# Two linear layers change places, the last attention slots run beside the first of them, and twelve modulation sums are dealt out anew

## The reference, cut to what matters

```
mod = c_act @ w_mod + b_mod                      # 3 x 2048 per layer: shift, scale, gate
h = rms_norm(x, g_norm) * (1 + scale) + shift
rq, rk, rv, rg, cq, ckv, kr, mg, bg = split(h @ w_in)
o_ret = head_group_norm(retention(rope(rq), rope(rk), rv))
y_ret = (o_ret * silu(rg)) @ w_ret_proj          # job "retproj"
q  = rms_norm(cq) @ w_uq ; kv = rms_norm(ckv) @ w_ukv
o_mla = mla_attention(q, kv, kr)                 # 16 heads
y_mla = (o_mla * silu(mg)) @ w_mla_proj          # job "mlaproj"
g_a, g_b = split(sigmoid(bg))                    # jobs "ga" and "gb0".."gb3"
x = x + gate * ((g_a * y_ret + g_b * y_mla) @ w_out)   # job "out"
```

## Time and profile before

| What | Value |
|---|---|
| Median of 3 runs | 3378.76 us (3378.43 to 3387.96) |
| The profiled execution | 3377.11 us, of which its span is 3375.4 us |
| PE busy | 3165.9 us, 94% of the span |
| DVE, ACT busy | 66%, 44% |
| Mean granted PE clock | 0.976 of full |
| Moved by DMA | 650.13 MB, mean 193 GB/s |

### The profile page before, as it was taken

One profiled execution on the slowest core, in us unless ns is written; L12 is line 12 of the kernel. 1 busy time (PEld: TensorE's weight loads), 2 busy tenths in 40 slices (PEclk: granted clock), 3 DMA queues, 4 the chain that ended last, 5 costly groups with the idle time before them and its releaser, 6 DMA issues. The chain is left out here.

```text
span 3375.4 us, 51760 instructions
## 1 busy us (share of the span) xinstructions
PE 3165.9 (94%) x20984; PEld 2734.9 (81%) x20984; DVE 2237.6 (66%) x2653; ACT 1480.8 (44%) x1843; POOL 108.0 (3%) x206
## 2 busy tenths in 40 slices
PE   6999997999989799999999999989999999999997
PEld 5898886878878688888877778868888887777886
DVE  7687877687674668677766667764555765565564
ACT  5454543344453333344444444433334544444443
POOL 0000000000000000000000000000000000000000
PEclk9999998999999899999999999989999999999999
DMA  5334764767544366656653467645544554344543
GB/s 209 127 112 147 260 245 167 280 249 264 187 160 153 145 219 256 235 213 242 244 187 134 149 250 288 217 181 176 179 157 162 188 199 173 127 150 176 212 175 112
DMA packets 102889, 650.13 MB, mean 193 GB/s; under 512 B 11552, under 2 KB 12704, under 8 KB 38688
## 3 DMA queue, kind: packets, MB, share of 16 engines
q1 hardware_dynamic: 71856, 512.44, 42.3%
q0 software_dynamic: 28528, 105.92, 8.7%
q10 hardware_dynamic: 2304, 28.84, 2.1%
HBM read 632.47 MB, written 14.68 MB: 192 GB/s over the span
## 5 line engine op out<-in xcount | busy, mean ns | idle before, releaser
L1562 PE MATMUL acc<-xs,whi 128*128 128x512 f32 x6960 | 2501.1, 403 | 76.3 <-DVE xs L983 60.2
L1564 PE MATMUL acc<-xs,wlo 128*128 128x256 f32 x6960 | 1957.1, 281 | 0.0
L1562 PEld LDWEIGHTS acc<-xs,whi 128*128 128x128 f32 x6960 | 1315.2, 189 | 407.5 <-issue 59.5
L903 DVE TENSOR_TENSOR wlo<-raw,whi 128x2048 fp32r<-128x2048 f32 x459 | 1051.8, 2292 | 502.0 <-ACT whi L444 501.4
L1564 PEld LDWEIGHTS acc<-xs,wlo 128*128 128x128 f32 x6960 | 1322.8, 190 | 6.2 <-issue 3.6
L444 ACT ACTIVATE whi<-raw 128x2048 fp32r<-128x2048 f32 x459 | 875.2, 1907 | 0.0
L468 ACT ACTIVATE acctmp<-acc 128x256 f32<-128x256 f32 x547 | 208.8, 383 | 1349.6 <-PE acc L1564 1331.4
L953 DVE TENSOR_TENSOR w<-acc,acctmp 128x256 f32<-128x256 f32 (+1 forms) x480 | 206.2, 430 | 462.9 <-ACT acctmp L468 462.3
L925 DVE SCALAR_TENSOR_TENSOR modacc<-modw,cact,modacc 128x1024 f32<-128x1024 f32 x192 | 245.6, 1279 | 16.0 <-DMA modw<-in_modstream 14.7
L423 POOL DMA_DIRECT2D modw<-in_modstream x192 | 101.5, 529 | 1709.7 <-DVE modacc L925 1037.4
L529 ACT ACTIVATE smx<-smx,stat 128x128 f32<-128x128 f32 x96 | 43.0, 448 | 175.6 <-DVE stat L1056 175.6
(11 more groups left out here) (256 smaller groups left out, 2181.9 us busy)
## 6 DMA issues: line engine op xcount, KB each, us to landing
raw<-in_wstream SPq DMA_DIRECT2D x483, 1024.0 KB, 4.8
modw<-in_modstream POOLq DMA_DIRECT2D x192, 512.0 KB, 4.7
residual<-h ACTq DMA_DIRECT2D x2, 2048.0 KB, 6.3
ga_gate<-w ACTq DMA_DIRECT2D x2, 2048.0 KB, 10.9
gated_retention<-w ACTq DMA_DIRECT2D x2, 2048.0 KB, 8.5
w<-gated_retention ACTq DMA_DIRECT2D x2, 2048.0 KB, 8.2
h<-residual ACTq DMA_DIRECT2D x2, 2048.0 KB, 12.6
w<-ga_gate ACTq DMA_DIRECT2D x2, 2048.0 KB, 11.3
```

The costliest lines, as they stand in the source:

```text
L903: dve.tensor_tensor(out=wlo[s % SPL][:, :], in0=raw[s % RAW][:, :], in1=whi[s % SPL][:, :].bitcast(F32), op=ALU.subtract).then_inc(w_lo_do ...
L1562: pe.matmul(acc[par % 2][0:cols, :], whi[w][:, c:c + cols], x_split[:, k, :, :], start=(k == 0), stop=False, skip_group_check=True)
L1564: mm = pe.matmul(acc[par % 2][0:cols, 0:T], wlo[w][:, c:c + cols], x_split[:, k, 0, :], start=False, stop=(k == kts - 1), skip_group_check ...
```

## The change

1. In both layers `retproj` stands ahead of `mlaproj` in the job list and in memory.
2. The gated retention comes back into `h`, the residual's buffer, from the start of `gb3`. `gb3` is now `held` and splits `retgated` ahead beside its last block.
3. Slots 15 to 17 run beside blocks 0 to 2 of `retproj`; `mlagated` is split ahead beside the last block of `retproj`.
4. The residual comes back into `h` at block 2 of `retproj`; `ga` comes back at block 5 in four loads of 512 KB into four buffers `ga_w` (on the space of the finished attention); the sigmoid of `gb` moves to blocks 6 to 9. The merge beside `mlaproj` first weights the retention result with `ga`, later adds the other one.
5. The 12 modulation chunks: `foxz` and layer 0's `rg` have none any more; layer 1's `rv` and `mg` have one each. Layer 0's `retproj` and `mlaproj` each keep one. The wait of the modulation matmuls on stored attention heads goes with `foxz`.

```
-              + [("mlaproj", 16), ("retproj", 16), ("out", 16)])
+              + [("retproj", 16), ("mlaproj", 16), ("out", 16)])
...
-MOD_JOBS = [(None, n) for n in ("glu", "s5out", "k", "v", "q", "foxz")] + \
-           [(0, n) for n in ("rv", "ga", "rg", "mg", "mlaproj", "retproj")]
+MOD_JOBS = [(None, n) for n in ("glu", "s5out", "k", "v", "q")] + \
+           [(0, n) for n in ("rv", "ga", "mg", "retproj", "mlaproj")] + [(1, "rv"), (1, "mg")]
...
+        ga_w = [at(f"ga_w{g}", [P, 4, T], F32, o) for g, o in enumerate((o_cr, o_cr + 4 * K, o_cr + 8 * K, o_stg))]
... ACT:
-                attend_slot(a0, MLA_H - 1, MLA_H)
-                attend_slot(a0, MLA_H, MLA_H)
-                act.wait_ge(acc_done, JOBS[(l, "mlaproj")][1])
-                for g in range(4):
-                    act.wait_ge(sem("att_stored"), a0 + 4 * g + 4)
-                    act.activation(xs[:, 4 * g:4 * g + 4, 0, :], group(w2)(g), ACT.Copy).then_inc(x_hi_done, 1)
...
+                act.dma_start(h[:, :, :], away["gated_retention"]).then_inc(sem("gated_back"), 16)
+                project((l, "gb3"), side=before_last(lambda j: attend_slot(a0, MLA_H - HG + j - 1, MLA_H), ret_early, HG - 1),
+                        held=True)
+                split_x(f"retgated{l}", group(h), xs, JOBS[(l, "retproj")][1], (3,))
+                split_held((l, "gb3"))
+                def back_side(j):
+                    if j < 2:
+                        attend_slot(a0, MLA_H - 1 + j, MLA_H)
+                    if j == 2:
+                        act.wait_ge(x_lo_done, SPLIT_BEFORE[f"retgated{l}"] + 4)
+                        act.dma_start(h[:, :, :], away["residual"]).then_inc(sem("residual_back"), 16)
+                    if j == 5:
+                        act.wait_ge(sem("att_stored"), a0 + MLA_H)
+                        act.wait_ge(sem("ga_away"), 16 * (l + 1))
+                        for g in range(4):
+                            act.dma_start(ga_w[g][:, :, :], group(away["ga_gate"])(g)).then_inc(sem("ga_back"), 16)
+                    if 6 <= j < 10:
+                        act.activation(group(w3)(j - 6), group(w3)(j - 6), ACT.Sigmoid).then_inc(sem("gb_gate"), 1)
... PE:
-            project((None, "foxz"), xs, side=fox_slot, before_mod=(sem("att_stored"), FOX_H - 2))
+            project((None, "foxz"), xs, side=fox_slot)
...
-                for k in range(MLA_H - 1, MLA_H + 2):
-                    mla_slot(k)
-                project((l, "mlaproj"), xs, fresh=f"mlagated{l}", before_mod=(sem("att_stored"), a0 + MLA_H), side=unrolled)
-                project((l, "retproj"), xs, fresh=f"retgated{l}", side=unrolled)
+                def slot_side(j):
+                    if j < 3:
+                        mla_slot(MLA_H - 1 + j)
+                project((l, "retproj"), xs, fresh=f"retgated{l}", side=slot_side, before_mod=(sem("att_stored"), a0 + MLA_H))
+                project((l, "mlaproj"), xs, fresh=f"mlagated{l}", side=unrolled)
```

More of the change, by code:

```diff
@@ L113 @@
 NSQUARES = {n: k for n, k, _ in NORMS}
-RELEASES = [(None, "glu"), (None, "f")] + [(l, n) for l in range(2) for n in ("mlaproj", "retproj")]
+RELEASES = [(None, "glu"), (None, "f")] + [(l, n) for l in range(2) for n in ("gb3", "retproj", "mlaproj")]
 OVER = {n: f for n, _, f in NORMS}
@@ L313, in released, with before_last @@
             return 3 * RELEASES.index(key) + g + 1
-        def before_last(side, early):
+        def before_last(side, early, last=KT - 1):
             def at_block(j):
@@ L319, in at_block @@
                     side(j)
-                if j == KT - 2:
+                if j == last - 1:
                     early()
@@ L867, in back_side @@
[L867 to L876, removed]
+                    if g < MLA_G - 1:
+                        project((l, f"gb{g}"), side=lambda j: attend_slot(a0, HG * g + j - 1, MLA_H))
@@ L877, in ret_early @@
                 def ret_early():
                     act.wait_ge(sem("gated_back"), 16 * (l + 1))
[L879 to L887, removed]
@@ L890, in _ @@
+                project((l, "retproj"), side=before_last(back_side, lambda: split_x(
+                    f"mlagated{l}", group(w2), xs, 0, range(3), (l, "retproj"))), held=True)
+                split_x(f"mlagated{l}", group(w2), xs, JOBS[(l, "mlaproj")][1], (3,))
+                split_held((l, "retproj"))
+                project((l, "mlaproj"), side=before_last(None, lambda: split_x(
+                    f"merged{l}", group(w1), xs, 0, range(3), (l, "mlaproj"))))
                 split_x(f"merged{l}", group(w1), xs, JOBS[(l, "out")][1], (3,))
@@ L1483, in ret_early @@
                 def ret_early():
-                    last_mod_step((l, "mlaproj"))
                     dve.wait_ge(sem("gated_back"), 16 * (l + 1))
                     for g in range(3):
-                        split_x(f"retgated{l}", group(w2), xs, g)
-                project((l, "mlaproj"), lambda j: tile(w1, j), side=before_last(None, ret_early), held=True)
-                split_x(f"retgated{l}", group(w2), xs, 3)
-                split_held((l, "mlaproj"))
-                dve.wait_ge(acc_summed, JOBS[(l, "retproj")][1])
+                        split_x(f"retgated{l}", group(h), xs, g)
@@ new lines, in _, with mla_early @@
+                project((l, "gb3"), lambda j: w3[:, MLA_H - HG + j, :],
+                        side=before_last(lambda j: mla_slot(MLA_H - HG + j - 1), ret_early, HG - 1), held=True)
+                split_x(f"retgated{l}", group(h), xs, 3)
+                split_held((l, "gb3"))
+                def mla_early():
+                    last_mod_step((l, "retproj"))
+                    for g in range(3):
+                        split_x(f"mlagated{l}", group(w2), xs, g)
+                def slot_side(j):
+                    if j < 3:
+                        mla_slot(MLA_H - 1 + j)
+                    if j == 3:
+                        dve.wait_ge(sem("att_stored"), a0 + MLA_H)
@@ L1493, in merge_side @@
+                project((l, "retproj"), lambda j: tile(w1, j), side=before_last(slot_side, mla_early), held=True)
+                split_x(f"mlagated{l}", group(w2), xs, 3)
+                split_held((l, "retproj"))
+                dve.wait_ge(acc_summed, JOBS[(l, "mlaproj")][1])
+                dve.wait_ge(x_lo_done, SPLIT_BEFORE[f"mlagated{l}"] + 4)
                 def merge_side(j):
+                    if j == 0:
+                        dve.wait_ge(sem("ga_back"), 64 * (l + 1))
                     if j < 4:
-                        dve.wait_ge(sem("gb_gate"), 4 * l + j + 1)
```

42 lines of the change are left out of this document (20 added, 22 removed).

## The result

The changed kernel takes 3351.62 us (median of 4 runs, 3350.19 to 3356.67) against 3378.60 (4 runs, 3375.82 to 3387.96): a ratio of 0.9913, 95% interval 0.9894 to 0.9932. The forecast was 3353, range 3343 to 3367.

A forecast was written before the change was run, and what follows sets the result against it. PE was busy 94% of the span, so gains were expected mainly where PE waits or runs at its lower clock. Terms -8.7 + 0.5 - 1.3 - 8.2 - 7.3 + 1.0 = -24.0 took 3377.1 to 3353 us, range 3343 to 3367.

The forecast's parts named there:

- Term 1: End of rg, layer 0: losing its modulation chunk removes PE's idle and lower clock; -8.7 us, ends -10 and -7.
- Term 2: rv and mg of layer 1: one added chunk each, hidden under blocks; +0.5 us for both, ends -1 and +3.
- The rival that the chunks cost 2 x 8.7 there: rv and mg, layer 1: moved chunks cost what rg's did, 2 x 8.7 us, giving 3370.0 us; chance 0.05.
- Term 3: End of foxz: without its chunk's modulation matmuls, slots 16 and 17 come earlier; -1.3 us, ends -3 and 0.
- Term 4: From gb3 to retproj's fourth block: attention's tail runs beside retproj; -8.2 us in layer 0, -7.3 in layer 1.
- Seams between the projections: Transitions retproj to mlaproj and mlaproj to out: same splits, held block and chunk as before; 0 us.
- pace: Plain blocks run at 5.55 or 5.65 us, cause unknown; small mean loss expected, +1.0 us, ends -5 and +5.
- The wait at the seam: Rival, gb3 to retproj: fourth group 4 us later, PE at lower clock for a block; 3364.7 us, chance 0.11.
- The late load: Rival, gb3: 2 MB retention load into h lands too late, slower than before; 3389 us at 49 us landing, chance 0.03.
- The faster pace: Rival: jobs behind the change fall into the 5.55 us block pace, giving 3345 us; chance 0.04.

The follow-up runs named there:

- the chunks alone: The kernel before with only the modulation chunks dealt out anew, mlaproj still ahead of retproj: 3371.11 us, ratio 0.9976.
- the tail alone: The changed kernel without part 5, so the modulation chunks stay where they were before: 3361.75 us, ratio 0.9951 to the kernel before.

## Why the prediction was right, point by point

**Term 1, -8.7: measured -8.6**, and -9.2 in the kernel with the chunks alone against the tail alone (150.9 and 160.1 us). Over all traces it is 150.3 to 150.9 us in the seven without the chunk, and 159.2 and 160.1 in the two that have it as before. The cause holds, too, and is shown by taking the wait away while the chunk stays; it is 6.3 of the 8.6.

**Term 2, +0.5: measured +1.0 in this trace.** From layer 1's last tile of rk to the last of ga it is

```profile
2349.64 0.38 ACT L469 ACTIVATE acctmp<-acc 128x256 f32<-128x256 f32 x1 [3.46 <-PE acc L1582]
...
2554.56 0.38 ACT L469 ACTIVATE acctmp<-acc 128x256 f32<-128x256 f32 x1 [5.28 <-PE acc L1582]
```

204.92 us, where it was 204.60. The rest is from kr to uq0's last tile, beside mg (109.7 for 109.1). Over all ten traces the first stretch is 204.6 to 204.9 with the chunk and 202.8 to 206.0 without, the second 107.2 to 109.7 with and 109.1 to 110.1 without, so no cost can be told from chance. The rival that the chunks cost 2 x 8.7 there is out.

**Term 3, -1.3: measured about -0.7**, and this is no clean test: the granted clock over 22 us there (from 1000) is 0.77 before and 0.84 after, but 0.77 again in the second trace of the change. The modulation matmuls at 1002.26 are gone, though PE now waits 1.73 us for slot 15's copies and 1.89 us for its probabilities; foxout's first tile comes 20.05 us behind foxz's last, where it was 21.94. Over all traces that lead is 21.94, 22.20 and 21.96 us with the chunk and 20.05 to 21.57 without, seven of them with a mean of 21.0: -1.0. The lead ahead of foxz was 0.4 us longer in the mean of the same seven, with no cause found.

**Term 4, -8.2 and -7.3: measured -8.9 and -7.8**, from ukv3's last copy, in sum 1.2 us better. It holds over the traces: from that copy to the projection's fourth, both layers take 63.3 to 63.6 us in the four traces with the new tail, and 71.2 to 72.2 in the three with the old one. The walk gave PE's wait at the fourth group as 1.3 us (measured 1.29) and 31.1 us to the fourth copy. Counted from where gb3's last copy would be without the splits ahead of it (1.3 us earlier: it comes 10.23 us behind the one before, where it was 8.90), 30.5 are measured. That both halves are needed is shown: without the early splits a layer costs 5 us more, without the slots beside the blocks 4 to 5.

**Seams between the projections, 0; pace, +1.0.** From the fourth copy to out's first, layer 0 gains another 3.0 us: two gaps between tiles before, one in mlaproj and one in retproj, were 0.84 and 1.11 us over the rest, and are gone, and twelve blocks run at 5.55 for 5.65. In layer 1 out's lead is 1.3 us longer (10.91 for 9.65) and its first gap 0.7 shorter; the second trace of the change has 9.66 there, so this, too, is chance (see the last section). Which pace a job comes out at changes between runs of one kernel (retproj of the change: 5.55 in one trace, 5.65 in the other), so no pair of traces tells this term from chance. It was the term without a mechanism, and the only one on the wrong side: against the sum of -24.0 the medians fell by 27.0 and 25.8 us.

**How near the number is** is in part luck. The sum missed by 3.0 us, but it was taken off the profiled execution, 3377.1 us, which lay 1.5 us under the median of its kernel, 3378.6; so 3353 came within 1.5 us of 3351.6, with the four runs of the change 6.5 us apart. The range is a little wider than its own rule: half of the spread from -39 to -7 gives some 3345 to 3362 us, the seam's case 3365, and 3343 to 3367 was stated.

**The rivals.** The wait at the seam didn't come, at 1.29 us with the clock at 1.00; made on purpose (no early split), it costs 10 to 12 us, and the rival's price was 11.6. The rule of the Trainium skill cited with it ("TensorE: Matmul & The Clock Gate", Part 1), by which half rate is the default and activity releases it, was no objection: the trace agrees with it where PE stood 3.31 us and more, and at 1.29 us nothing fell. Between them waits of 2.07 to 2.25 us went both ways (last section). The late load was ruled out by 22 us of room (31 - 9.0), and its price of one for one is measured (8.01 us of wait, 8.2 and 7.9 of job). The chunks in layer 1 cost nothing that counts. The faster pace was there in some jobs and not in others.

**The signs.** Those of being right are there: cq's first tile is 5.54 us behind rg's last, no modulation matmuls stand at foxz's end, PE's wait for the fourth split is under 2 us in both layers (1.29 and 1.30). Those of being wrong are absent: ACT's early splits start without a wait for the load, PE waits over 1 us for none of layer 1's modulation matmuls, and the clock is 1.00 across the seam from retproj to mlaproj in both layers.

**What stays open** is why a plain block runs at 5.55 or 5.65 us, and what sets it for a whole job; and why three of ten profiled executions have 3.3 to 3.6 us more in the first projection (nearly all of it in its first two gaps between tiles, 10.56 and 10.73 us in the change's trace for 9.05 and 8.60 before). Neither was tried.

## What to carry to other kernels

Where PE idles at the end of a job, look at what the late engine does last and in which order: a 1.28 us step behind a 3.35 us reciprocal cost 4.77 us and then a stretch at the lower clock, and a move cured it, not less work; then look for the same fault at the next job, which here was worth another 5.4 us. Where a profile has a job twice, once with side work and once without, the difference is its price, here to within a microsecond or two of chance. Where the next projection's input hangs on the work that is just ending, put first the projection whose input is there already, split most of it early, and lay the remaining small work between its blocks.

## What the runs showed of the hardware

The clock falls or holds at the same wait. In the first block of the last projection (out of layer 1) PE waits for the fourth group of its input; its first matmul behind that wait, in the kernel before:

```profile
3265.01 0.50 PE L1562 MATMUL acc<-xs,whi 128*128 128x512 f32 x1 [2.07 <-DVE xs L983]
```

and after:

```profile
3243.95 0.79 PE L1580 MATMUL acc<-xs,whi 128*128 128x512 f32 x1 [2.08 <-DVE xs L987]
```

Behind 2.07 us the matmul takes 0.50 us, behind 2.08 it takes 0.79, and the first tile comes 1.3 us later. That nothing in the program makes the difference shows in the second trace of the very same changed kernel:

```profile
3240.98 0.50 PE L1580 MATMUL acc<-xs,whi 128*128 128x512 f32 x1 [2.07 <-DVE xs L987]
```

The length of the last wait alone thus doesn't decide it, and a seam with such a wait varies by more than a microsecond with nothing changed. The 2.25 us ahead of uq1, uq2 and uq3 are the same within one trace: in layer 0 before, the first matmul behind them takes 0.50, 0.80 and 0.50 us. The second surprise are the two paces of a plain block, 5.55 and 5.65 us. In retproj and mlaproj one of them holds from block to block for nearly the whole job and can be the other in the next run of the same kernel; in rg of layer 1 both stand in one job (5.65, 5.66, then 5.55, 5.55). Over a job of 16 blocks that is 1.6 us, over several jobs as much as a whole term of this prediction.
